# Weights split into high and low part: GpSimd's subtraction in pieces of 256 columns in place of one of 1024

## The chip, the cores and the metric

One core of a Trainium2 chip. The metric is the device time of one execution in microseconds. Five engines take part: TensorE (PE in the profile) with its own loader of weights (PEld), VectorE (DVE), ScalarE (ACT), GpSimd (POOL) and SyncE (SP, here only a queue of transfers).

## The reference, cut to what matters

The model is a chain of two blocks on 512 tokens of width 1024: two layers that mix a short convolution with a retention of four heads and have a wide MLP, and after them one layer of neighbourhood attention with a gated convolutional MLP. Nearly all of the work is in dense products in float32:

```python
proj = h @ w_in
...
return (b * z) @ w_out              # convolution mixer
...
return (jax.nn.silu(g) * o) @ w_out # retention mixer
...
x = x + merged @ w_o
h2 = rmsnorm(x, norm_mlp)
return x + jnp.square(jax.nn.relu(h2 @ w_up)) @ w_down
```

The second block adds `q`, `k`, `v`, `w_o`, `w_up` and `w_down` of the attention layer in the same manner.

## The kernel before, in words

Each float32 operand of a dense product is kept as two float32r parts, a high part (a rounded copy) and a low part (the operand minus its high part), and a product is three matmuls: high by high, high by low and low by high (`product`, line 465 on; the matmul itself is L468). Activations live in SBUF with features on the 128 partitions, in tiles of 128x512. Weights come as a stream of 404 blocks of 128x1024, each worth one job of TensorE: eight tiles of 128x128, so 24 matmuls of 512 columns into one PSUM bank.

The stream runs through a ring of four slots (`RING`), with a slot each in `w_raw`, `w_hi` and `w_lo`. For every block:

1. SyncE loads it into `w_raw` (L381) once the low part of the block four earlier is done (`w_lo_ready`).
2. ScalarE makes `w_hi` with a copy of 128x1024 (`ahead`, L864), once the block is loaded and TensorE has finished the job that used the slot (`jobs_done`).
3. GpSimd makes `w_lo` as `w_raw` minus `w_hi` (`low`, L421), once ScalarE has signalled `w_hi_ready`. This is one instruction of 128x1024 with both inputs in SBUF, and it signals `w_lo_ready`.
4. TensorE's `job` waits for `w_lo_ready` and for a free bank (`bank_free`), and runs.

So when a job ends, its slot goes through ScalarE and then GpSimd, and is wanted by TensorE three jobs later.

VectorE works on what TensorE leaves in PSUM. Between stages it splits activations: `split` casts the high part (L1117) and subtracts it (L1119), with a drain ahead of each. TensorE waits for each such tile (`tiles_ready`). Its other long stretches are: the angles of the rotary embedding at the start (L1179 to L1206), the centring and splitting of the values (L1232 to L1237), the rotary embedding of queries and keys (L1252 to L1258), the gated normalisation after retention (L1277 to L1284), the squares for the norms (L1131 to L1135), the norms (L1140 to L1148), products for the modulation of the attention layer beside the MLP (L1355, L1358), and in the last block the scaled additions of L1579 and L1615.

GpSimd has one more kind of work, in the attention layer alone: `head_biases` (L444), three subtractions of 192, 256 and 192 columns in a row with both inputs in SBUF, 16 times.

The engines' queues are written out by hand and each runs in order. There are 404 calls of `low`, most in loops over rounds of four, and 25 or so written out around the attention.

Of the kernel before, what the change touches and what calls it, by code (L numbers as in the profile page):

```python
# [22 lines left out]
F32 = mybir.dt.float32  # L23
# [3 lines left out]
ALU = mybir.AluOpType  # L27
AX_X = mybir.AxisListType.X

P = 128  # L30
# [4 lines left out]
EPS = 1e-6  # L35
RING = 4
BLK = DT * P


RH, RQK, RV = 4, 128, 256  # L40
# [137 lines left out]
def build(nc, x, ctx_in, weights, mod_weights, params, positions, decay, key_mask, rpb, block_ones, ident, out):  # L178
# [4 lines left out]
    with ctx:  # L183
# [6 lines left out]
        def at(name, offset, shape, dt=F32):  # L190
            return nc.alloc_sbuf_tensor_at(name, [P, *shape], dt, offset=base + offset)

        def pair(name, offset):

            return (at(name + "_hi", offset, [DT, S], F32R), at(name + "_lo", offset + 16 * KB, [DT, S], F32R),
                    at(name + "_hi_f", offset, [DT, S]), at(name + "_lo_f", offset + 16 * KB, [DT, S]))
# [5 lines left out]
        C_hi, C_lo, Cf, Clf = pair("C", 112 * KB)  # L202
        w_raw = at("w_raw", 144 * KB, [RING, BLK])
        w_hi = at("w_hi", 160 * KB, [RING, BLK], F32R)
        w_lo = at("w_lo", 176 * KB, [RING, BLK], F32R)
        decay_sb = at("decay_sb", 192 * KB, [RH, S])
# [13 lines left out]
        ctx_acc = at("ctx_acc", 106 * KB, [MOD_CTX, P])  # L220
        mod_w = at("mod_w", 80 * KB, [MOD_GROUP, BLK])
        ST = at("ST", 112 * KB, [3, 2, S], F32R)
# [51 lines left out]
        w_lo_ready = sem("w_lo_ready")  # L274
# [141 lines left out]
        @block.gpsimd  # L416
        def _(pool):
            def low(n, q):

                pool.wait_ge(w_hi_ready, n + 1)  # L420
                nc.gpsimd.tensor_tensor(w_lo[:, q, :], w_raw[:, q, :], w_hi[:, q, :].bitcast(F32),  # L421
                                        ALU.subtract).then_inc(w_lo_ready, 1)

            def low_rounds(first, last):
                with pool.Fori(first, last) as i:
                    for q in range(RING):
                        low(i * RING + q, q)

            low_rounds(0, ATT_ROUND)

            def head_biases(head):


                if head < 2:
                    pool.wait_ge(bias_cleared, 1)
                pool.wait_ge(toep_loaded[head % 2], (head // 2 + 1) * 16)
                if head >= BIAS_SLOTS:
                    T, a = divmod(head - BIAS_SLOTS, 2)
                    pool.wait_ge(min_ready, 2 * STEPS * T + 2 * (STEPS - 1) + a + 1)
                for kind in range(3):  # L440
                    n = REAL_KEYS[kind]
                    o = (head % BIAS_SLOTS) * BIAS_LEN + kind * KEYS + REAL[kind].start
                    t = TOEPLITZ_OFF[kind]
                    last = nc.gpsimd.tensor_tensor(  # L444
                        bias[:, o:o + n], mask_sb[:, MASK_OFF[kind]:MASK_OFF[kind] + n],
                        toeplitz[:, head % 2, t:t + n], ALU.subtract)
                last.then_inc(bias_ready, 1)

            for n in range(ATT_JOB, ATT_JOB + 3):
                low(n, n % RING)  # L450
            pool.wait_ge(late_loaded, 16 * LATE)
            for T in range(TILES):
                n = ATT_JOB + 3 * T + 3
                low(n, n % RING)
                head_biases(2 * T)
                low(n + 1, (n + 1) % RING)
                head_biases(2 * T + 1)
                low(n + 2, (n + 2) % RING)
            low(WO_JOB + 3, 3)
            low_rounds(WO_ROUND + 1, ROUNDS)  # L460
# [1291 lines left out]
```

## Time and profile before

| what | value |
|---|---|
| median of three runs | 2637.7 us (2637.61, 2637.70, 2646.06) |
| the profiled execution, its own time | 2645.72 us |
| its span (first to last instruction) | 2643.9 us |
| granted TensorE clock, mean of the span | 0.974 |
| busy share of the span: PE, DVE, ACT, POOL | 94%, 61%, 31%, 39% |
| chain that ended last, by engine | PE 78%, DVE 15%, DVEq (drains) 3%, ACT 2%, issue 2% |
| HBM traffic over the span | 93 GB/s |

The profiled execution is one run, and 8.0 us above the median. Times below are from its trace, in microseconds from the start of the span. A row of a timeline has the start, the duration, the engine, the line, the operation and its operands, and in brackets how long the engine had been idle and what ended that. A duration of VectorE or GpSimd runs from the instruction's start to its end, and holds whatever it waited for once it had started.

### The profile page before, as it was taken

How to read it: one execution, taken by the hardware profiler on the slowest of the kernel's cores; microseconds unless marked ns; L12 is line 12 of the kernel's file. 1: busy time of each engine (PE TensorE's matmuls, PEld its weight loads, DVE VectorE, ACT ScalarE, POOL GpSimd, SP SyncE). 2: the span in 40 equal slices, each digit the busy share in tenths (PEclk: the TensorE clock that was granted, in tenths of full speed). 3: DMA queues.
4: the chain of work that ended last, by engine and by line, in shares of the span. 5: the costliest groups of instructions: out<-in, count | busy, mean ns of one | idle time of the engine just before them, and what ended most of it. 6: DMA issues, size and time to landing. Idle time of an engine off the chain costs nothing.

```text
span 2643.9 us, 32621 instructions
## 1 busy us (share of the span) xinstructions
PE 2488.3 (94%) x11368; PEld 2014.9 (76%) x11368; DVE 1612.3 (61%) x1793; ACT 814.4 (31%) x1076; POOL 1040.1 (39%) x456
## 2 busy tenths in 40 slices
PE   6789999989999987999999899999599998799999
PEld 4677888868888876778888688888377776588887
DVE  7965154477666878732544776668866654763534
ACT  3132222222222221322222222222367774332222
POOL 3314444434444433244444344444123223244443
PEclk9989999999999998999999999999699999899999
DMA  4202222223433322122222323333111111132322
GB/s 158 80 31 89 95 96 97 100 95 121 143 143 117 119 76 78 43 92 96 95 97 97 123 95 143 140 138 113 35 47 56 47 39 64 64 103 89 102 93 89
DMA packets 64440, 247.24 MB, mean 94 GB/s; under 512 B 7152, under 2 KB 9584, under 8 KB 63088
## 3 DMA queue, kind: packets, MB, share of 16 engines
q1 hardware_dynamic: 62064, 218.92, 24.0%
q10 hardware_dynamic: 2304, 27.38, 2.7%
q8 instruction: 43, 0.70, 0.1%
q14 instruction: 29, 0.24, 0.0%
HBM read 244.17 MB, written 2.10 MB: 93 GB/s over the span
## 4 chain that ended last, share of the span: by engine, by line
PE 78%; DVE 15%; DVEq 3%; ACT 2%; issue 2%; DMA 0%; ACTq 0%
PE ps L468 73%; DVE E L1135 2%; PE ps L705 1%; PE ps L692 1%; DVE C_lo_f L1284 1%; DVE C_lo L1119 1%; DVE E L1131 1%; PE ps L721 1%; DVEq L1278 1%; DVE A_lo L1119 1%; DVE A_hi L1117 1%; PE ps L660 1%; DVE H_lo_f L1143 1%; DVE C_hi L1117 1%; DVEq L1256 1%
## 5 line engine op out<-in xcount | busy, mean ns | idle before, releaser
L421 POOL TENSOR_TENSOR w_lo<-w_raw,w_hi 128x1024 fp32r<-128x1024 f32 x404 | 1010.2, 2503 | 1563.5 <-ACT w_hi L864 1422.0
L468 PE MATMUL ps<-H_hi,w_hi 128*128 128x512 f32 x1952 | 781.8, 401 | 33.6 <-DVE H_lo L1442 14.6
L468 PE MATMUL ps<-H_lo,w_hi 128*128 128x512 f32 x1952 | 766.8, 393 | 0.0
L468 PE MATMUL ps<-H_hi,w_lo 128*128 128x512 f32 x1952 | 766.6, 393 | 0.0
L864 ACT ACTIVATE w_hi<-w_raw 128x1024 fp32r<-128x1024 f32 x401 | 422.6, 1057 | 842.4 <-PE ps L468 800.2
L468 PEld LDWEIGHTS ps<-H_hi,w_hi 128*128 128x128 f32 x1952 | 370.3, 190 | 133.4 <-issue 45.6
L468 PEld LDWEIGHTS ps<-H_hi,w_lo 128*128 128x128 f32 x1952 | 370.5, 190 | 79.0
L468 PEld LDWEIGHTS ps<-H_lo,w_hi 128*128 128x128 f32 x1952 | 370.9, 190 | 76.2 <-issue 3.6
L468 PE MATMUL ps<-A_hi,w_hi 128*128 128x512 f32 x560 | 220.9, 394 | 5.8 <-DVE A_lo L1119 4.2
L468 PE MATMUL ps<-A_hi,w_lo 128*128 128x512 f32 x560 | 218.7, 391 | 0.0
L468 PE MATMUL ps<-A_lo,w_hi 128*128 128x512 f32 x560 | 218.7, 391 | 0.0
L468 PE MATMUL ps<-C_hi,w_hi 128*128 128x512 f32 x384 | 150.1, 391 | 4.5 <-DVE C_lo L1119 4.5
L468 PE MATMUL ps<-C_lo,w_hi 128*128 128x512 f32 x384 | 149.4, 389 | 0.0
L468 PE MATMUL ps<-C_hi,w_lo 128*128 128x512 f32 x384 | 149.4, 389 | 0.0
L1358 DVE SCALAR_TENSOR_TENSOR mod_w<-mod_w,cond 128x768 f32<-128x768 f32 x56 | 146.9, 2624 | 0.0
L1119 DVE TENSOR_TENSOR A_lo<-A_lo_f,A_hi x78 | 141.5, 1814 | 5.8
L468 PEld LDWEIGHTS ps<-A_hi,w_hi 128*128 128x128 f32 x560 | 105.5, 188 | 32.0 <-DVE A_lo L1119 7.6
L468 PEld LDWEIGHTS ps<-A_hi,w_lo 128*128 128x128 f32 x560 | 105.5, 188 | 22.4
L468 PEld LDWEIGHTS ps<-A_lo,w_hi 128*128 128x128 f32 x560 | 105.6, 189 | 21.1
L880 ACT ACTIVATE E<-ps 128x512 f32<-128x512 f32 x64 | 38.3, 598 | 240.8 <-PE ps L468 240.8
L1117 DVE CAST A_hi<-A_lo_f x78 | 99.3, 1273 | 13.2 <-issue 9.0
L1292 DVE TENSOR_TENSOR A_lo_f<-B_hi_f,ps 128x512 f32 x16 | 11.0, 687 | 148.3 <-PE ps L468 148.3
(214 smaller groups left out, 3081.1 us busy)
## 6 DMA issues: line engine op xcount, KB each, us to landing
w_raw<-weights SPq DMA_DIRECT2D x404, 512.0 KB, 3.5
mod_w<-mod_weights ACTq DMA_DIRECT2D x8, 3072.0 KB, 10.5
X<-x SPq DMA_DIRECT2D x4, 512.0 KB, 6.8
out<-X SPq DMA_DIRECT2D x8, 256.0 KB, 2.0
toeplitz<-biases SPq DMA_DIRECT2D x14, 128.0 KB, 2.2
decay_sb<-decay ACTq DMA_DIRECT2D x1, 1024.0 KB, 7.5
ctx_sb<-context SPq DMA_DIRECT2D x1, 1024.0 KB, 5.4
mask_sb<-key_mask ACTq DMA_DIRECT2D x1, 320.0 KB, 2.7
```

The source lines that it names most:

```text
L421: nc.gpsimd.tensor_tensor(w_lo[:, q, :], w_raw[:, q, :], w_hi[:, q, :].bitcast(F32), ALU.subtract).then_inc(w_lo_ready, 1)
L468: mm = nc.tensor.matmul(dst, w[l], xs[r], start=start and a == 0, stop=stop and a == 2)
L660: nc.tensor.matmul(dst, block_sb[:, :], src[:, :], start=True, stop=True).then_inc(sum_ready[kind], 1)
L692: mm = nc.tensor.matmul(ps[:, SCORE_BANKS[head], :], (q_hi, q_lo)[l][rows, T % 2, i * P:(i + 1) * P], (k_hi, k_lo)[r][rows, first:first + ...
L705: mm = nc.tensor.transpose(ps[:, TURN_BANK, c * P:(c + 1) * P], prob[:, head, at_col:at_col + P], ident_sb[:, :])
L721: nc.tensor.matmul(ps[cols[head], OUT_BANK, o0:o0 + 2 * P], v_sb[:, T % 2, tile, cols[head]], pt[:, head, c, :, :].rearrange("p t n -> p ( ...
L864: nc.scalar.activation(w_hi[:, s, :], w_raw[:, s, :], ACT.Copy).then_inc(w_hi_ready, 1)
L880: nc.scalar.activation(dst, ps[:, q, :], func).then_inc(ev_ready, 1)
L1117: V.tensor_copy(hi, whole)
L1119: V.tensor_tensor(lo, whole, hi.bitcast(F32), ALU.subtract).then_inc(ready, 1)
L1135: return V.tensor_tensor(E[:, SUMSQ, :], E[:, SUMSQ, :], E[:, 0, :], ALU.add)
L1358: step = V.scalar_tensor_tensor(out=acc, in0=mod_w[:, 0:tiles, k * P:(k + 1) * P], scalar=cond[:, k, who:who + 1], in1=acc, op0=ALU.mult, ...
```

## The change

The loop in `low` issues four subtractions of 256 columns for each block, one after the other with nothing between them, and only the last one signals `w_lo_ready`. What is computed, the order of the blocks and every wait stay as they were.

```diff
+LOW_COLS = 2 * P
...
             def low(n, q):
 
                 pool.wait_ge(w_hi_ready, n + 1)
-                nc.gpsimd.tensor_tensor(w_lo[:, q, :], w_raw[:, q, :], w_hi[:, q, :].bitcast(F32),
-                                        ALU.subtract).then_inc(w_lo_ready, 1)
+                for c in range(0, BLK, LOW_COLS):
+                    last = nc.gpsimd.tensor_tensor(w_lo[:, q, c:c + LOW_COLS], w_raw[:, q, c:c + LOW_COLS],
+                                                   w_hi[:, q, c:c + LOW_COLS].bitcast(F32), ALU.subtract)
+                last.then_inc(w_lo_ready, 1)
```

## Rows read from the trace of the kernel before

**Rows 1.** Page, part 1: busy time, share of the span, instructions of an engine.

```profile
PE 2488.3 (94%) x11368; PEld 2014.9 (76%) x11368; DVE 1612.3 (61%) x1793; ACT 814.4 (31%) x1076; POOL 1040.1 (39%) x456
```

**Rows 2.** Groups of GpSimd's instructions by shape: busy us, mean ns, idle before.

```profile
L421 POOL TENSOR_TENSOR w_lo<-w_raw,w_hi 128x1024 fp32r<-128x1024 f32 x404 | 1010.2, 2503 | 1563.5 <-ACT w_hi L864 1422.0 <-DVE stat L1505 123.3 <-ACT w_hi L896 18.1
...
L444 POOL TENSOR_TENSOR bias<-mask_sb,toeplitz 128x256 f32<-128x256 f32 x16 | 11.9, 743 | 0.0
```

**Rows 3.** Waits of TensorE: us in total, times, longest us.

```profile
PE ps L468 <- DVE A_lo L1119: 33.3, 10, 16.0
...
PE ps L490 <- DVE E L1135: 11.5, 3, 6.5
...
PE ps L468 <- POOL w_lo L421: 1.6, 1, 1.6
```

**Rows 4.** One line's instructions: durations in ns, min/median/max.

```profile
L421 POOL TENSOR_TENSOR w_lo<-w_raw,w_hi x404: 2329/2402/2946, 12.8 to 2625.6; 128x1024 fp32r<-128x1024 f32 x135
L1119 DVE TENSOR_TENSOR A_lo<-A_lo_f,A_hi x78: 691/2722/2735, 99.3 to 2608.3; - x78
```

**Rows 5.** Timeline around 720 us, at a change of stage in an MLP.

```profile
719.79 2.66 POOL L421 TENSOR_TENSOR w_lo<-w_raw,w_hi 128x1024 fp32r<-128x1024 f32 x1 [2.78 <-ACT w_hi L864]
...
720.27 2.73 DVE L1119 TENSOR_TENSOR C_lo<-C_lo_f,C_hi  x1
...
723.05 0.50 PE L468 MATMUL ps<-C_hi,w_hi 128*128 128x512 f32 x1 [0.17 <-DVE C_lo L1119]
```

**Rows 6.** Timeline, attention layer: GpSimd's three bias subtractions beside VectorE, and each alone.

```profile
1925.35 2.26 POOL L444 TENSOR_TENSOR bias<-mask_sb,toeplitz 128x192 f32<-128x192 f32 x3
1925.76 0.53 DVE L1117 CAST k_hi<-k_lo_f 128x256 fp32r<-128x256 f32 x1
1926.36 0.80 DVE L1119 TENSOR_TENSOR k_lo<-k_lo_f,k_hi 128x256 fp32r<-128x256 f32 x1
...
1942.36 0.29 DVE L1117 CAST k_hi<-k_lo_f 128x256 fp32r<-128x256 f32 x1
1942.72 0.43 DVE L1119 TENSOR_TENSOR k_lo<-k_lo_f,k_hi 128x256 fp32r<-128x256 f32 x1
...
1964.87 1.30 POOL L444 TENSOR_TENSOR bias<-mask_sb,toeplitz 128x256 f32<-128x256 f32 x2
```

**Rows 7.** Timeline of the first layer up to the retention.

```profile
36.36 2.55 DVE L1181 TENSOR_SCALAR C_hi_f<-C_hi_f,par 128x512 f32<-128x512 f32 x1
...
74.01 2.39 POOL L421 TENSOR_TENSOR w_lo<-w_raw,w_hi 128x1024 fp32r<-128x1024 f32 x1 [2.87 <-ACT w_hi L864]
...
76.87 0.68 DVE L1232 TENSOR_REDUCE small<-ps 128x2 f32<-128x512 f32 x1
...
116.28 2.02 DVE L1117 CAST A_hi<-A_lo_f  x1 [0.52 <-issue]
...
136.67 0.79 PE L468 MATMUL ps<-A_hi 128*128 128x512 f32 x1 [15.98 <-DVE A_lo L1119]
```

**Rows 8.** Timeline of the second layer up to the retention.

```profile
1037.48 1.78 DVE L1258 TENSOR_TENSOR A_lo_f<-C_hi_f 128x512 f32 x1 [0.20 <-issue]
...
1053.72 0.80 PE L468 MATMUL ps<-A_hi 128*128 128x512 f32 x1 [13.13 <-DVE A_lo L1119]
```

**Rows 9.** Timeline of TensorE at two other changes of stage.

```profile
231.02 0.50 PE L468 MATMUL ps<-C_hi,w_hi 128*128 128x512 f32 x1 [1.93 <-DVE C_lo L1119]
...
2611.11 0.50 PE L468 MATMUL ps<-A_hi,w_hi 128*128 128x512 f32 x1 [1.69 <-DVE A_lo L1119]
```

**Rows 10.** Timeline of the attention's output projection.

```profile
2233.49 2.86 DVE L1131 TENSOR_TENSOR E<-X 128x512 f32<-128x512 f32 x1
...
2235.75 2.85 POOL L421 TENSOR_TENSOR w_lo<-w_raw,w_hi 128x1024 fp32r<-128x1024 f32 x1
...
2235.86 0.50 PE L468 MATMUL ps<-A_hi,w_hi 128*128 128x512 f32 x1 [1.62 <-POOL w_lo L421]
...
2264.43 2.07 PE L490 MATMUL ps<-E,ones 128*128 128x512 f32 x2 [6.47 <-DVE E L1135]
```

## The prediction

> **What bounds the kernel now.** I read the shares of the engines first. TensorE is busy for 2488 of 2644 us, GpSimd for 39% of them [rows 1]. So at most some 155 us can be won without touching the matmuls, and a longer GpSimd has room. Then I read who TensorE waits for. GpSimd is named in one wait of its matmuls, of 1.6 us; VectorE in nearly all, as in 33.3 us for the split L1119 and 11.5 us for the sum of squares [rows 3]. What the change makes longer is almost never waited for; what may matter is what it does to VectorE.
>
> The third view, the durations of one line, shows that link. The split's subtraction takes 691 ns at best and 2722 in the median [rows 4]. The timeline shows why: GpSimd starts a subtraction at 719.79, VectorE's starts at 720.27 and ends at 723.00, 0.55 after GpSimd's end [rows 5]. VectorE stood for 2.04 us. This holds all through the trace for VectorE's casts and for its operations with two SBUF inputs; those that read PSUM keep their time. Nothing but GpSimd's w_lo lies at such places, so GpSimd's 2.4 us instruction holds something that these operations need. The question is what four short ones do to that.
>
> **GpSimd's side.** One of 1024 columns takes 2402 ns in the median [rows 4], one of 256 of the same kind 743 [rows 2]. In a row they overlap by some 0.05: the bias pair of 256 and 192 columns takes 1.30 [rows 6]. So four take 3 x 0.69 + 0.74 = 2.81, 0.41 more. Over 404 blocks that is 166 us of GpSimd, 39% to 46% busy. A block's slot is free one job ahead of the next three, about 16.3 us at 5.44 us a job; ScalarE (1.06) and GpSimd (2.81, with VectorE's operations between perhaps 4.5) use 5.6 of them. Behind the later `w_lo_ready` stand SyncE's load, as far ahead, and in the attention layer the next biases. The added time is hidden by that lead. It shows only where the ring has run dry: at 2235.86, where TensorE waits for the first block of the output projection [rows 10], and once ahead of the last attention steps.
>
> **VectorE's side: what a wait becomes.** The nearest rows are the three bias subtractions in a row, of 192, 256 and 192 columns [rows 6]. VectorE's cast at 1925.76 takes 0.53 there and 0.29 alone, its subtraction at 1926.36 takes 0.80 and 0.43 alone. The waits are 0.24 and 0.37, both ended while GpSimd was still within its three (until 1927.61). So a waiting VectorE gets in between two queued GpSimd instructions. The same is seen with w_lo itself: VectorE's L1131, started at 2233.49, ends at 2236.35, inside the w_lo that had followed at 2235.75 without a gap, and that one took 2.85 in place of 2.40 [rows 10]. I take 0.35 for each operation that meets a piece, with up to three or four met during a block: 0.35 where one waits, 0.7 to 1.0 in a dense row, against 2.04 now. The bounds are 0.2 (the cast's) and 0.7 (a whole piece each time; four then cost 2.8, more than now).
>
> **Where this reaches TensorE.** Only delays on VectorE work that TensorE ends up waiting for count. A stop of TensorE costs its idle time and about 0.27 for the slower first starts (after 723.05 [rows 5] the next comes at 723.39, where 0.227 is the rule, and the idle column leaves out part of the gap).
>
> - First layer, to the retention. VectorE works without a break from 35.9 to 136.6, with 16 such delays from the first to the last one shown [rows 7], 29.7 us in all. But the second half of the values can't start before TensorE's eighth job ends, at 72.9 (the w_lo of 74.01 less ScalarE's 1.06), or about 71.6 with 1.3 won on the first norm; VectorE now comes to it at 76.87. From there seven delays of 11.7 us become 6.0, at 0.75 for each of the eight blocks that still come. So 5.3 + 5.7 = 11. TensorE's wait of 16 us covers it.
> - Second layer, the same place. VectorE is continuous from 997.1 only, with seven delays of 9.1 us up to the one shown [rows 8]. They become about 4: 5 us, out of a wait of 13.1.
> - Gated normalisation, twice. Delays of 12 us become about 6, but TensorE loses only 1.93 + 0.27 [rows 9]: 2.2 each, 4.4.
> - MLP, eight changes from up to down: 0.17 + 0.27 [rows 5], all won, since the last tile comes 1.7 earlier: 3.5. The two changes to `w_o` have 0.28 idle: 1.1.
> - Last MLP: three changes with 1.28, 0.35 and 1.69 idle (the last one in [rows 9]), where cast and subtraction both wait for GpSimd: 1.55 + 0.62 + 1.96 = 4.1.
> - The norms. In the last MLP group of either layer VectorE comes 0.45 late to the final addition: 0.9. The norms themselves have no w_lo beside them, the ring being full: nothing.
> - Output projection. VectorE is continuous from 2232.2 to 2264.4 with 11.6 us of delays. TensorE's first job starts later, by 0.41 and by VectorE's operations let in between, 1.2 together; its last ends near 2259, and three undisturbed operations (1.15 + 0.69 + 0.69) lead to 2262 in place of 2264.4 [rows 10]: 2.4 won.
> - Ahead of the last attention steps: 0.5 lost.
>
> The sum is 11 + 5 + 4.4 + 3.5 + 1.1 + 4.1 + 0.9 + 2.4 - 0.5 = 31.9. The profiled execution took 2645.7 and would take 2613.8. The median is 8.0 below it, and the same parts hold there: 2637.7 - 31.9 = 2605.8. What is late next is VectorE's own arithmetic in the first and second layer, and TensorE elsewhere.
>
> **Two rules of the Trainium skill.** That VectorE stands until GpSimd's instruction ends is what the page "SBUF — State Buffer", section "SBUF: two separate sides", calls an exclusive lock on a shared pair of ports, held for the whole instruction; the trace agrees (2.73 for 0.69 in [rows 5]). The page "GPSIMD Engine Reference", section "2.1 Instruction dispatch", speaks against the change: a core of GpSimd starts the next instruction as soon as its own share of the last is done, so four in a row might never let go. By it the first rival below would come true; the 0.24 and 0.37 of [rows 6] speak against it.
>
> **The rivals.**
> *No gap (slower).* GpSimd's four pieces hold VectorE out from the first to the last. Each wait is then 0.41 longer than now. On the path there are 16 + 7 in the first two layers, 6 and 6 in the normalisations (their slack is gone already), 16 in MLP changes and others, 7 at the output projection: some 50 x 0.41 = 20 less some that is hidden, 15 us: 2653. It decides wherever a waiting VectorE isn't served between pieces. For it: a w_lo is written as float32r and its pieces may follow more tightly than the biases. Against it: both cases above. 0.08.
> *Every piece costs a whole piece.* VectorE gets in but waits 0.6 to 0.7 each time. In dense rows three or four waits cost 2.0 to 2.8, as now; only single waits and changes of stage win: 0 to 3 of the 16 in the two early layers, about 2 of the normalisations, 8 at the changes, 1 at the projection, in all 12 to 18. 2622. For it: 0.69 is the distance of starts. Against it: the waits read were half of that. 0.20.
> *Something else is late instead.* VectorE's waits shrink, but TensorE's place is taken by the ring: GpSimd's block with let-in operations passes 5.44 us, or TensorE's bank comes from ScalarE. Then only the changes of stage remain, 5 to 8 us: 2631. For it: GpSimd alternates with VectorE in the densest stretches. Against it: 2.81 + 3 x 0.5 is 4.3. 0.07.
> *The forecast*, 24 to 40 us won: 0.65.
>
> **How the numbers follow.** A measurement of this kernel tells about 0.5%, 13.2 us, from no change. Faster: 0.65 and 0.12 of the second rival, which lies across that bound, 0.77. Same: the rest of it and most of the third, 0.14. Slower: the first, with what is left, 0.09. The range goes from 2596 (waits of 0.2, and the early layers winning 8 more) to 2630, which takes in the second rival.
>
> **What would show it.** L1119's median should fall from 2722 to near 1050, casts and L1135 likewise. GpSimd's 1616 pieces should come 0.69 apart where alone, its busy share near 46%. TensorE's wait before the retention should fall from 16.0 to about 5 and from 13.1 to 8; those at 231 and at the changes of the MLPs should vanish. I would be wrong if L1119 stayed at 2.7 or above, or if TensorE began to wait for w_lo in the steady stretches.

## The result, and the profile after

The changed kernel takes 2606.0 us in the median of four runs (2605.4 to 2606.8), the kernel before 2637.7 beside it: a ratio of 0.9873, with a 95% interval of 0.9853 to 0.9893. Of the 31.7 us won, 31.9 had been forecast. The sum is right; two of its terms are not, and that they cancel is luck.

The runs of the kernel before are not all alike, and what follows rests on that. They fall into two groups, of 2637 to 2641 and 2643 to 2647 us (24 and 16 of the 40 runs made beside the kernels of this study). The execution that stands ahead of the prediction belongs to the upper group. The changed kernel's eight runs lie within 2602.9 to 2606.8.

The page of the changed kernel, of its parts 1, 4 and 5 (line numbers are 3 higher than before: the subtraction of the split is L1122, the matmul L471, GpSimd's w_lo L423):

```profile
PE 2477.2 (95%) x11368; PEld 2012.5 (77%) x11368; DVE 1242.3 (48%) x1793; ACT 814.9 (31%) x1076; POOL 1373.0 (53%) x1668
...
PE 88%; DVE 7%; issue 2%; DVEq 2%; ACT 1%; POOL 0%; DMA 0%; ACTq 0%; POOLq 0%
...
L423 POOL TENSOR_TENSOR w_lo<-w_raw,w_hi 128x256 fp32r<-128x256 f32 x1616 | 1343.2, 863 | 1193.8 <-ACT w_hi L867 1057.6
```

VectorE does the same 1793 instructions in 370 us less than in [rows 1], and GpSimd needs 333 us more. The chain now runs through VectorE for 7% of the span, where it was 15%. The durations of the split's subtraction, min/median/max in ns, answer to [rows 4]:

```profile
L1122 DVE TENSOR_TENSOR A_lo<-A_lo_f,A_hi x78: 691/1070/1079, 89.4 to 2569.8; - x78
```

And TensorE's waits (us in total, times, longest us) answer to [rows 3]:

```profile
PE ps L471 <- DVE A_lo L1122: 17.5, 2, 9.0
...
PE ps L493 <- DVE E L1138: 9.1, 5, 2.7
PE ps L540 <- ACT A_lo_f L937: 4.3, 2, 2.2
...
PE ps L471 <- POOL w_lo L423: 2.7, 1, 2.7
```

The ten waits for `A_lo` have become two, the ones ahead of the two retentions. The six for `C_lo` (4.5 us in all before) and the one for `B_lo` (0.3) are gone. In the timeline these two are, with the start of the output projection's second half and the norm behind it:

```profile
123.24 0.80 PE L471 MATMUL ps<-A_hi 128*128 128x512 f32 x1 [8.95 <-DVE A_lo L1122]
...
1026.70 0.79 PE L471 MATMUL ps<-A_hi 128*128 128x512 f32 x1 [8.50 <-DVE A_lo L1122]
...
2204.53 0.50 PE L471 MATMUL ps<-A_hi,w_hi 128*128 128x512 f32 x1 [2.68 <-POOL w_lo L423]
...
2229.35 1.15 PE L493 MATMUL ps<-E,ones 128*128 128x512 f32 x2 [2.72 <-DVE E L1138]
```

The prediction calls the block waited for at this place the first of the output projection. It is the fifth of its eight: the first four are multiplied ahead, inside the attention (`WO_AHEAD`), and TensorE waits when it comes to the next round of the ring.

A change of stage in an MLP, the place of [rows 5], now looks like this:

```profile
699.30 3.90 POOL L423 TENSOR_TENSOR w_lo<-w_raw,w_hi 128x256 fp32r<-128x256 f32 x4 [1.91 <-ACT w_hi L867]
699.77 1.07 DVE L1122 TENSOR_TENSOR C_lo<-C_lo_f,C_hi  x1
```

The subtraction of 0.69 us waits 0.38 for the piece in hand, not 2.04 for the block, and TensorE no longer stops there. The four pieces take 3.90 beside VectorE.

### The profile page after: what moved, and what is told of

It is laid out like the page before. It is cut to its first block, busy times and chain, and to the rows that moved or that the text cites. A ratio compares the mean times of both kernels' runs of the same rounds, so it can differ in the third digit from the quotient of the medians.

```text
span 2603.8 us, 33833 instructions
## 1 busy us (share of the span) xinstructions
PE 2477.2 (95%) x11368; PEld 2012.5 (77%) x11368; DVE 1242.3 (48%) x1793; ACT 814.9 (31%) x1076; POOL 1373.0 (53%) x1668
## 4 chain that ended last, share of the span: by engine, by line
PE 88%; DVE 7%; issue 2%; DVEq 2%; ACT 1%; POOL 0%; DMA 0%; ACTq 0%; POOLq 0%
PE ps L471 83%; PE ps L695 1%; PE ps L708 1%; DVEq L1259 1%; PE ps L724 1%; PE ps L663 1%; DVE H_lo_f L1439 1%; DVE E L1143 1%; DVE A_lo_f L1261 0%; DVE H_lo_f L1146 0%; DVE C_hi_f L1257 0%; DVE H_lo L1151 0%; DVE H_lo L1445 0%; DVE C_hi_f L1256 0%; PE ps L728 0%
## 5 line engine op out<-in xcount | busy, mean ns | idle before, releaser
L423 POOL TENSOR_TENSOR w_lo<-w_raw,w_hi 128x256 fp32r<-128x256 f32 x1616 | 1343.2, 863 | 1193.8 <-ACT w_hi L867 1057.6
L471 PE MATMUL ps<-H_hi,w_hi 128*128 128x512 f32 x1952 | 779.4, 399 | 31.3 <-DVE H_lo L1151 14.8
L471 PE MATMUL ps<-H_lo,w_hi 128*128 128x512 f32 x1952 | 764.0, 391 | 0.0
L471 PE MATMUL ps<-H_hi,w_lo 128*128 128x512 f32 x1952 | 764.0, 391 | 0.0
L471 PEld LDWEIGHTS ps<-H_hi,w_hi 128*128 128x128 f32 x1952 | 368.5, 189 | 128.8 <-issue 39.7
L471 PEld LDWEIGHTS ps<-H_hi,w_lo 128*128 128x128 f32 x1952 | 368.9, 189 | 78.4
L471 PEld LDWEIGHTS ps<-H_lo,w_hi 128*128 128x128 f32 x1952 | 369.5, 189 | 75.8 <-issue 3.6
L471 PE MATMUL ps<-A_hi,w_hi 128*128 128x512 f32 x560 | 220.0, 393 | 2.7 <-POOL w_lo L423 2.7
L471 PE MATMUL ps<-A_hi,w_lo 128*128 128x512 f32 x560 | 218.9, 391 | 0.0
L471 PE MATMUL ps<-A_lo,w_hi 128*128 128x512 f32 x560 | 218.8, 391 | 0.0
L471 PE MATMUL ps<-C_hi,w_lo 128*128 128x512 f32 x384 | 149.4, 389 | 0.0
L471 PE MATMUL ps<-C_hi,w_hi 128*128 128x512 f32 x384 | 149.4, 389 | 0.0
L471 PE MATMUL ps<-C_lo,w_hi 128*128 128x512 f32 x384 | 149.4, 389 | 0.0
L1163 DVE TENSOR_TENSOR X<-X,ps 128x512 f32<-128x512 f32 x80 | 55.0, 688 | 171.2 <-PE ps L471 171.2
L471 PEld LDWEIGHTS ps<-A_hi,w_hi 128*128 128x128 f32 x560 | 105.6, 189 | 25.9 <-POOL w_lo L423 3.1
L471 PEld LDWEIGHTS ps<-A_hi,w_lo 128*128 128x128 f32 x560 | 105.5, 188 | 22.2
L471 PEld LDWEIGHTS ps<-A_lo,w_hi 128*128 128x128 f32 x560 | 105.6, 189 | 21.5
L1361 DVE SCALAR_TENSOR_TENSOR mod_w<-mod_w,cond 128x768 f32<-128x768 f32 x56 | 84.1, 1502 | 0.0
L471 PEld LDWEIGHTS ps<-C_hi,w_hi 128*128 128x128 f32 x384 | 72.1, 188 | 15.1
L471 PEld LDWEIGHTS ps<-C_lo,w_hi 128*128 128x128 f32 x384 | 72.1, 188 | 14.9
```

The source lines that it names most:

```text
L423: last = nc.gpsimd.tensor_tensor(w_lo[:, q, c:c + LOW_COLS], w_raw[:, q, c:c + LOW_COLS], w_hi[:, q, c:c + LOW_COLS].bitcast(F32), ALU.sub ...
L471: mm = nc.tensor.matmul(dst, w[l], xs[r], start=start and a == 0, stop=stop and a == 2)
L1163: add = V.tensor_tensor(X[:, m, :], X[:, m, :], ps[:, q, :], ALU.add)
L1361: step = V.scalar_tensor_tensor(out=acc, in0=mod_w[:, 0:tiles, k * P:(k + 1) * P], scalar=cond[:, k, who:who + 1], in1=acc, op0=ALU.mult, ...
```

## The experiments

**1. The kernel before, once more.** No edit.

> The kernel before, unchanged, looked at once more: its profiled execution was 8 us above its median, and the two profiles stand 40.1 us apart where the medians stand 31.7 apart. Theory: those 8 us are TensorE's granted clock, which in the first profile fell to 1.2 GHz again at 173, at 231 and at 1146 us while TensorE had work; a run near 2637.6 lacks at least one of these stretches, has a mean clock near 0.978 and reaches the gated stage's end (the C_lo wait, 231.0 in the first profile) at most 1 us earlier relative to the retention's start other than by clock. Rival: the 8 us lie in VectorE's waits for GpSimd, which fall differently from run to run; then the clock rows are the same and the wait before the retention (16.0 us) or the sum of L1119's durations differs by several us. If the run comes out near 2646 again, the trace should repeat the first one to within 1 us at every stage.

It took 2638.5 us, span 2636.6, of the lower group. The timeline of TensorE, and the busy time of the engines in the stretch up to the retention (us, then busy us and instructions of PE, PEld, DVE, ACT and POOL, granted clock, DMA), first of this run and then of the execution shown ahead of the prediction:

```profile
131.00 0.79 PE L468 MATMUL ps<-A_hi 128*128 128x512 f32 x1 [13.26 <-DVE A_lo L1119]
...
0.00:131.00 131.00, 92.08 (x386) 74.44 (x386) 107.89 (x138) 34.35 (x38) 47.20 (x23) 0.97 0.34 120
```

```profile
0.00:136.67 136.67, 91.78 (x387) 73.18 (x387) 114.44 (x138) 34.11 (x38) 47.35 (x23) 0.95 0.32 115
```

The same 138 instructions of VectorE hold 6.6 us more of waiting in the execution that the prediction was read from, and its retention begins 5.7 later. The two run alike up to 41 us; then GpSimd's next block starts at 41.43 in the one and at 42.82 in the other, and from there VectorE's operations meet the blocks at other points. The two spans differ by 7.3 us, so the rest of the program makes only 1.6. The theory of the expectation, the clock, was wrong in the main, and its rival, VectorE's waits, explains most. The half clock at 173 us is indeed missing in this run, and the stretch from the retention to the next norm is 2.2 us shorter; 0.6 of that come back later.

**2. Two pieces, and eight.** `LOW_COLS` at 512 and at 128.

```diff
-LOW_COLS = 2 * P
+LOW_COLS = 4 * P
```

```diff
-LOW_COLS = 2 * P
+LOW_COLS = P
```

> Two subtractions of 512 columns for each block in place of four of 256. If VectorE gets in between two instructions of GpSimd and waits for what is left of the one that runs, a wait becomes 0.6 to 1.0 us (L1119's median 1.3 to 1.7 us against 2.7 before and about 1.06 with four), the MLPs' changes of stage win all they won, the early layers win about half: 20 to 27 us below the kernel before, 2611 to 2618. If only the presence of any gap counted and not its spacing, it would be as with four, 2606. If nothing got in between (the no-gap rival), it would be at or above 2638.

> Eight subtractions of 128 columns for each block. Each is some 0.45 us from start to start, so 3.5 us a block alone, against 2.8 with four and 2.4 with one: GpSimd near 62% busy. Theory: a single wait falls to about 0.2 us and up to six are met in a dense row, so a block costs VectorE 0.8 to 1.2 in dense stretches, no less than with four: 2604 to 2609, L1119's median below 0.95. Rival (each piece costs a whole piece whatever its size, so finer cuts keep winning): under 2600. Rival (the ring becomes the bound): TensorE waits for w_lo in the steady stretches and the time goes above 2612.

Two pieces took 2624.6 us, ratio 0.9946 (0.9929 to 0.9962): 13.7 won where 20 to 27 were expected, a miss. In its profile 4.3 of these lie between the last attention step and the last norm, where TensorE also had a better clock (1.00 in place of 0.66 for 10 us, see experiment 3). Eight took 2605.9, ratio 0.987 (0.9853 to 0.9886), as expected and no better than four. The stretch up to the retention in two pieces, in four and in eight, with the split's subtraction above it for two and for eight:

```profile
L1122 DVE TENSOR_TENSOR A_lo<-A_lo_f,A_hi x78: 691/1622/1628, 93.5 to 2588.5; - x78
...
0.00:129.21 129.21, 90.99 (x386) 73.69 (x387) 104.76 (x138) 34.23 (x38) 55.34 (x42) 0.96 0.35 122
```

```profile
0.00:123.24 123.24, 90.96 (x386) 73.65 (x387) 97.07 (x138) 34.24 (x38) 66.83 (x80) 0.98 0.36 127
```

```profile
L1122 DVE TENSOR_TENSOR A_lo<-A_lo_f,A_hi x78: 691/793/797, 87.7 to 2569.5; - x78
...
0.00:120.63 120.63, 91.56 (x386) 74.12 (x386) 88.01 (x138) 34.34 (x38) 84.08 (x156) 0.99 0.37 130
```

The wait of one subtraction is 2.03 us for blocks of 1024 columns, 0.93 for 512, 0.38 for 256 and 0.10 for 128. GpSimd's instructions take 2.40, some 1.27 (the shortest), 0.70 (the distance of starts) and 0.42 (experiment 4): each wait is one instruction less about a third of a microsecond. That is why two pieces disappoint. Where VectorE works without a break it meets every piece: 2 x 0.93 is still 1.86 of the 2.03 for each block, 4 x 0.38 is 1.5, 8 x 0.10 is 0.8. VectorE's busy time up to the retention falls accordingly, 107.9, 104.8, 97.1, 88.0. At a change of stage a single wait counts, and there two pieces are enough: the stops in the MLPs of the two layers are gone in that kernel, while those of the gated normalisation stay:

```profile
220.74 0.50 PE L471 MATMUL ps<-C_hi,w_hi 128*128 128x512 f32 x1 [1.76 <-DVE C_lo L1122]
```

Eight pieces bring the retention 2.6 us earlier than four, and by the first norm of the attention layer (the matmul that waits 15.63 for L1177) they are 4.7 ahead, 1837.78 against 1842.52. They lose it behind that, where TensorE waits for other engines (a product in the norm of the keys, and the output projection):

```profile
1870.34 2.08 PE L663 MATMUL ps<-sq_k,block_sb 128*128 128x512 f32 x2 [3.68 <-ACT sq_k L1008]
...
2203.20 0.56 PE L471 MATMUL ps<-A_hi,w_hi 128*128 128x512 f32 x1 [4.14 <-POOL w_lo L423]
```

The first of these is no price of the pieces. ScalarE has this tile ready 32.4 to 32.6 us behind the first norm in every profile, with whole blocks too; a TensorE that comes earlier waits longer (1.75 with four pieces, 1.97 in the repeated kernel before). What is lost is the clock: behind the 3.68 the next eight matmuls start 0.43 us apart in place of 0.23. The same is in the mixed kernel of experiment 5, with whole blocks in this layer and 3.67 here, and not in its sister with 2.27. From the first norm to the last attention step the two with the drop take 347.5 us, the sister 344.8 and the repeated changed kernel 345.6. The second wait is GpSimd's price: a block in eight pieces beside VectorE comes 1.5 us later than in four, at the one place where the ring has run dry. Behind it the clock is 0.69 for 5.5 us where it is 1.00 in the repeated changed kernel, and the norm behind comes 1.6 later still. These three parts, 1.9, 1.5 and 1.6, are the whole lead, and only the second is GpSimd's time.

**3. One stretch at a time.** Each kernel has whole blocks everywhere but in one stretch of the stream. `low_rounds` got the number of columns as an argument, and `low` makes a whole block where none is given:

```diff
-            low_rounds(0, ATT_ROUND)
+            low_rounds(0, JOB_G // RING + 1, LOW_COLS)
+            low_rounds(JOB_G // RING + 1, ATT_ROUND)
```

```diff
-            low_rounds(0, ATT_ROUND)
+            LR = LAYER_JOBS // RING
+            low_rounds(0, 5)
+            low_rounds(5, 9, LOW_COLS)
+            low_rounds(9, LR + 5)
+            low_rounds(LR + 5, LR + 9, LOW_COLS)
+            low_rounds(LR + 9, ATT_ROUND)
```

```diff
-            low_rounds(WO_ROUND + 1, ROUNDS)
+            low_rounds(WO_ROUND + 1, ROUNDS, LOW_COLS)
```

> Four pieces for the first 20 blocks alone (values, queries and keys of the first layer, and the first four after them), one piece for the other 384. By the two profiles the start of the first layer's retention comes 13.4 us earlier (136.67 to 123.24), of which 2.3 lie ahead of the first product; if the delays of VectorE there are the cause, all of it is had by these 20 blocks: 12.5 to 14.5 us less than before, some 2624, and after it the waits at the MLPs' changes (0.16 to 1.9 us) are all there again. If the gain came from something that the pieces do to the whole program (fewer drops of the clock, less traffic), it would be under 5 us.

> Four pieces of 256 columns for the 16 blocks around the gated normalisation of each of the two layers and nowhere else; every other block has one instruction of 1024. This prices the term of the gated normalisations by itself. Theory of the prediction (waits of TensorE alone): 1.93 + 0.27 in each layer, 4.4 us, less because the first norm and the first layer keep their delays: 2633 to 2634. Rival found in the traces (the stop also costs the clock): the 3.4 us at half clock that stand right behind the stop in the first profile, at 231 and at 1146, and in the repeated one, at 223 and 1138, go as well, 1.7 us each: 7.8 us, 2629 to 2631. If the waits in these places are only partly gone, because the blocks before keep VectorE late, less than 3 us are won and the half-clock stretches stay.

> Four pieces of 256 columns from the second round of the output projection to the end (the last MLP with its norm), one instruction of 1024 everywhere before. By the lead that the changed kernel gained between the norm before the last MLP and its end (4.06), and the net gain at the output projection (1.65, of which the later start of its first block is not in this kernel, so 2 to 3): 6 to 7 us won, 2631 to 2632.5. The prediction's own terms for this part are 4.1 and 2.4, 6.5 us. The rival: the gains at the end exist only because earlier stages shifted the phase between VectorE and GpSimd; then less than 4 us are won and stops of over 1 us stay in the last MLP.

*The first 20 blocks*: 2630.7 us, ratio 0.9967 (0.9955 to 0.998), 7.7 won where 12.5 to 14.5 were expected, a miss: the expectation counted from the execution with the late retention. The retention begins at 123.40, as in the changed kernel, 7.6 ahead of the repeated kernel before. The six runs lie within 2630.4 to 2632.1. In all seven kernels of this study with pieces in these blocks, 34 runs, those of one kernel lie within 1.3 to 5.5 us; the two below with whole blocks there scatter over 9.0 and 13.5, as the kernel before does over 9.6. So the upper group comes from these blocks.

*The gated normalisations*: 2632.3 us, ratio 0.9979 (0.9966 to 0.9993). This interval goes from 1.8 to 9 us and separates nothing, but the traces do. From the start of the retention to the norm behind it, the repeated kernel before takes 434.96 us in the first layer and 435.07 in the second; this one 431.11 and 431.42; the changed kernel 430.35 and 431.39. So 3.7 to 3.9 are won in each layer, where TensorE's stop is 1.94 + 0.27. The medians are 6.5 us apart, between the 4.4 and the 7.8 of the two expectations. The rest is TensorE's clock. In the repeated kernel before:

```profile
223.16 0.50 PE L468 MATMUL ps<-C_hi,w_hi 128*128 128x512 f32 x1 [1.94 <-DVE C_lo L1119]
...
224.19 0.39 PE L468 MATMUL ps<-H_lo,w_hi 128*128 128x512 f32 x1
...
225.10 0.63 PE L468 MATMUL ps<-H_lo,w_hi 128*128 128x512 f32 x1
...
223.10:228.60 5.50, 5.44 (x17) 4.32 (x18) 0.69 (x2) 1.06 (x1) 2.36 (x1) 0.69 0.07 28
```

Right behind the stop the matmuls run at 0.39 us, then at 0.63, and the granted clock of the 5.5 us is 0.69: 3.4 of them are at 1.2 in place of 2.4 GHz (2 x 0.31 x 5.5), which costs half of that, 1.7. 17 matmuls are done in them, where 26 fit into the same time in the kernel with pieces in these places:

```profile
217.00:222.50 5.50, 5.50 (x26) 4.56 (x25) 1.71 (x3) 1.61 (x2) 2.95 (x4) 1.00 0.34 119
```

The kernel with two pieces shows the two parts by themselves, since it has the same stop twice, of 1.76 and 1.75 us, in the first layer with the drop of the clock behind it and in the second without:

```profile
220.70:226.20 5.50, 5.46 (x17) 4.34 (x18) 0.69 (x1) 1.06 (x1) 2.51 (x2) 0.69 0.19 76
1135.10:1140.60 5.50, 5.48 (x24) 4.56 (x25) 0.69 (x1) 1.06 (x1) 2.54 (x2) 1.00 0.20 80
```

Seven matmuls of 0.23 us are the clock's part, 1.6 us. The stop of 1.9 had it in both layers of both profiles of the kernel before, and again in both layers of the other two kernels of this experiment, which keep it; that of 1.69 at the end of the last MLP had not (24 matmuls, clock 1.00). So a stop of this length can cost the clock or not, and what decides is not shown; removing it takes the risk away.

*The output projection and the last MLP*: 2634.4 us in the median, 4.4 under that of the kernel before; 7.1 by the ratio, 0.9973 (0.9959 to 0.9987), which compares the means. 6 to 7 were expected. Both kernels scatter over 9 us, so the whole times say little, and the profiled execution is one with a late retention (137.11). None of the last MLP's stops is left. But it too waits 2.68 for w_lo in the output projection, as in the changed kernel: contrary to what the expectation says, the block waited for is the first of the loop that was changed. The whole span from the last attention step (the matmul with 2.96 idle) to the end takes 423.4 to 423.5 in four profiles with whole blocks there, 414.4 in this one, 416.7 and 415.6 in two profiles of the changed kernel. From the last norm to the end the three profiles with pieces agree to 0.1 us (374.4). What differs is the clock right behind the last attention step, ahead of the first block in pieces; the repeated kernel before, then this one:

```profile
2213.22:2223.22 10.00, 9.31 (x43) 6.26 (x44) 1.38 (x2) 1.76 (x3) 0.00 (x0) 0.66 0.01 2
2218.21:2228.21 10.00, 9.31 (x55) 7.20 (x56) 2.46 (x3) 2.77 (x5) 0.00 (x0) 1.00 0.01 2
```

At 1.00 the waiting block of the output projection starts 13.6 us after that step although it waits longer for w_lo; it is 15.4 in the kernel before and 16.4 and 17.5 in the changed one (clock 0.66 and 0.54). Here the clock falls behind the wait of 2.68 instead (0.69 for 5.5 us), and the norm comes 26.4 us later in place of 24.8. Most of the gain is given back so, and 1.2 of the 9.0 us are the clock's.

**4. The wait by itself.** A small kernel: GpSimd subtracts 8 blocks of 1024 columns in one go, in instructions of 1024, 256 or 128 columns, while VectorE makes 24 operations of 128x512.

```python
for i in range(8):
    for c in range(i * 1024, (i + 1) * 1024, cols):
        f = c % 1024
        last = nc.gpsimd.tensor_tensor(low[:, c:c + cols], a[:, f:f + cols], b[:, f:f + cols], ALU.subtract)
```

> It computes nothing of the reference: thirteen short phases in which GpSimd subtracts 8 blocks of 1024 columns in a row, in instructions of 1024, 256 or 128 columns, while VectorE makes 24 operations of 128x512, each drained or back to back, with both inputs in SBUF, with one in PSUM, or as a cast. Theory (a waiting VectorE gets in at the end of the GpSimd instruction in hand): beside instructions of 1024 VectorE's subtraction takes up to 2.4 + 0.69, about 2.8 to 3.1 in the mean; beside 256 columns 1.0 to 1.4; beside 128 columns 0.8 to 1.1; one with an input in PSUM keeps 0.69 and lets GpSimd keep its 0.74. Back to back operations of VectorE give the same, since GpSimd gets in between them too. Rival 1 (no gap): the first subtraction of VectorE beside 256 columns lasts until all 32 pieces are done, over 15 us. Rival 2 (a whole piece each time): 0.69 + 0.69, 1.38 in each. GpSimd's own price, without VectorE: 2.4 for 1024, 0.74 for 256 with starts 0.69 apart, and by the line through these two some 0.46 for 128, starts 0.4 apart.

GpSimd alone, with 1024, 256 and 128 columns (busy us, mean ns; the third phase is 27.0 us for 64 instructions):

```profile
L59 POOL TENSOR_TENSOR low<-a,b 128x1024 f32<-128x1024 f32 x8 | 18.9, 2395 | 8.3 <-DVE own L69 8.3
...
L59 POOL TENSOR_TENSOR low<-a,b 128x256 f32<-128x256 f32 x32 | 22.4, 750 | 0.1
...
L59 POOL TENSOR_TENSOR low<-a,b 128x128 f32<-128x128 f32 x64 | 27.0, 510 | 0.1
```

Both at once, VectorE subtracting in SBUF with a drain behind each (us; busy us and instructions of DVE, of POOL; clock, DMA), in the same order:

```profile
77.39:111.60 34.21, 32.45 (x24) 22.07 (x8) 1.00 0.00 0
111.62:144.30 32.68, 24.95 (x24) 32.63 (x32) 1.00 0.00 0
144.36:181.70 37.34, 18.74 (x24) 37.26 (x64) 1.00 0.00 0
```

Beside 256 columns one subtraction of VectorE takes 24.95 / 24 = 1.04, a wait of 0.35, which is the value that the prediction had taken. Beside whole blocks only eight of the 24 can meet one, at 2.68 by that estimate ((32.45 - 16 x 0.69) / 8), so the mean is 1.35 where 2.8 to 3.1 had been expected. Beside 128 columns it is 0.78. Without the drains the mean is 1.21 for 256 columns, a wait of 0.5. With an input in PSUM nothing waits on either side:

```profile
L59 POOL TENSOR_TENSOR low<-a,b 128x256 f32<-128x256 f32 x32 | 21.9, 731 | 0.1
L79 DVE TENSOR_TENSOR own<-ps,vb 128x512 f32<-128x512 f32 x24 | 16.6, 692 | 7.7 <-POOL low L59 6.0
```

The casts beside 256 columns take 0.80 in the mean and 0.43 alone, so they wait 0.37. No operation waited for a run of pieces (rival 1), and the mean waits stay below a whole piece of 0.70 (rival 2). The price is on GpSimd's side, and it is more than the three starts: beside a busy VectorE eight blocks take 22.1 us whole, 32.6 in 256 columns and 37.3 in 128. What VectorE no longer waits, GpSimd waits, a little each time.

**5. Mixed, and the first round of the output projection.** First with `low_rounds(0, ATT_ROUND, P)`, so pieces of 128 columns ahead of the attention, whole blocks in the attention layer and 256 columns behind it. Then the changed kernel again, together with two that have whole blocks for the last four blocks of the output projection as well, the round that TensorE waits for (the expectations call it the first):

```diff
-            low_rounds(WO_ROUND + 1, ROUNDS)
+            low_rounds(WO_ROUND + 1, WO_ROUND + 2)
+            low_rounds(WO_ROUND + 2, ROUNDS, LOW_COLS)
```

The first of these two is not the changed kernel with four blocks altered, as its expectation says: its 28 blocks made inside the attention layer are whole as well.

> A version meant to beat both: pieces of 128 columns up to the attention layer, one instruction of 1024 inside the attention layer and for the first blocks of the output projection, pieces of 256 columns after. By the leads read in the two changed kernels: the two retentions win 2.6 and 2.5 over pieces of 256, the start of the output projection loses nothing of the 2.1 that whole pieces lost there. If these parts add, 2599 to 2602. If what is won on VectorE in the early layers is given back in clock or in ScalarE's and the ring's waits, as with 128 everywhere, 2604 to 2607.

> The changed kernel itself once more, beside the two versions of this set. If its gain belongs to the change and not to one lucky profile: 2604 to 2608, and the retention of the first layer again begins at about 123.2. The profile of the changed kernel had 10 us at half clock around the start of the output projection where three others had 7, which made that start 1.0 later; if that is luck of one execution, the distance from the last attention step (the matmul with 2.96 idle) to the first matmul of the output projection is 16.4 here and not 17.5.

> The changed kernel with one instruction of 1024 columns kept for the four blocks of the first round of the output projection, where the ring has run dry and TensorE waits for the first block (2.68 us in place of 1.62). If GpSimd's added time costs there and nowhere else: that wait is 1.62 again and the matmul starts 1.06 earlier; but VectorE, which ends this stage, then waits for whole instructions again, so at most 1.1 us are won at the end and as much may be lost (in the kernel before, TensorE waited 6.5 for the norm's squares behind it, in the changed one 2.7). Time within 1.5 us of the changed kernel.

> Pieces of 128 columns up to the attention layer, whole instructions in it and for the first round of the output projection, pieces of 256 after. If the parts add, it is the gain of pieces of 128 in the two early layers (2.2 by the medians of the run with them) and up to 1.1 for the first round: 2601 to 2604. If the first round gives nothing: 2603 to 2605.

The mixed kernel took 2603.7 us (2599.8 to 2604.8), ratio 0.9857 (0.984 to 0.9875), between the sum of the parts and the other case. It too had the whole wait of 2.68 in the output projection, since the block waited for was in pieces.

The changed kernel again: 2606.2 us (2602.9 to 2606.8), its retention at 123.30. From the last attention step to the output projection it is 2204.80 - 2188.39 = 16.4, as expected, and not 17.5: the 1.1 was the clock of one execution (0.54 and 0.66 in the 10 us behind that step).

Pieces of 256 columns with whole blocks from the attention layer to the end of the output projection:

```profile
2203.57 0.50 PE L472 MATMUL ps<-A_hi,w_hi 128*128 128x512 f32 x1 [1.62 <-POOL w_lo L423]
...
2229.78 1.61 PE L494 MATMUL ps<-E,ones 128*128 128x512 f32 x2 [4.12 <-DVE E L1139]
```

The attention layer takes as long as in the repeated changed kernel (345.5 and 345.6 us from its norm to its last step), so its whole blocks changed nothing there. The matmul that waited comes 1.0 earlier after the last attention step (15.4 against 16.4), and the norm's first matmul comes 1.4 later behind it (26.2 against 24.8), since VectorE ends this stage and waits for whole blocks again. The time is 2608.3 us (2606.5 to 2609.0), 2.1 more than the changed kernel beside it where at most 1.5 either way was expected. So the later w_lo costs TensorE 1.06 there, and it is a good bargain.

The mixed kernel with this round whole took 2600.9 us (2600.2 to 2601.5), ratio 0.9842 (0.982 to 0.9863), 5.2 less than the changed kernel beside it, and no run of the one reaches the other. 2601 to 2604 had been expected if the parts add. At the first norm of the attention layer it leads by 4.45 (1838.31 against 1842.76). The whole round can't be what wins the rest, since by itself it lost a little. The profile has another source: the waiting matmul comes 13.75 us after the last attention step, and 15.39 with the same blocks in the kernel just shown, at a granted clock of 0.83 and 0.66 in the 10 us behind that step. Whether the other three runs had that clock isn't shown. Small pieces where VectorE works without a break ahead of TensorE are thus what beats four pieces everywhere; that whole blocks behind the attention help is not shown.

## Why the prediction was right, point by point

The lead of the changed kernel over the repeated kernel before, by TensorE's first matmul at each place, and what the steps of the prediction had for it:

Each row is the length in us from the place in the row above.

| stretch | before | after | won | forecast |
|---|---|---|---|---|
| start to first retention | 131.00 | 123.24 | 7.8 | 11 |
| to the norm behind it | 434.96 | 430.35 | 4.6 | 2.75 (gated 2.2, `w_o` 0.55) |
| to second retention | 480.64 | 473.11 | 7.5 | 7.2 (MLP 1.76, norm 0.45, retention 5) |
| to the norm behind it | 435.07 | 431.39 | 3.7 | 2.75 |
| to the last attention step | 731.55 | 728.97 | 2.6 | 1.7 (MLP 1.76, norm 0.45, less 0.5) |
| to the norm of the last block | 43.94 | 42.29 | 1.65 | 2.4 |
| to the end of the span | 379.44 | 374.45 | 5.0 | 4.1 |
| sum | 2636.6 | 2603.8 | 32.8 | 31.9 |

**The mechanism and its price** were right. The wait of the split's subtraction is 0.35 to 0.38 and not the 0.2 or 0.7 of the bounds; L1122's median is 1070 ns where near 1050 was forecast. The casts are where the row read was low: 0.24 for the narrow cast in [rows 6], 0.37 for one of 512 columns in experiment 4.

**First layer: the term was mis-sized against the median**, 11 where 7.8 came. The step that failed is the sentence on the 8.0 us between the profiled execution and the median, "and the same parts hold there". 5.7 of the 8.0 lay in just this part. Against the execution it was read from, 13.4 us were won. The start of the second half of the values divides what is left; it was 76.87 in [rows 7], and is, in the repeated kernel before and in the changed one:

```profile
74.26 0.69 DVE L1232 TENSOR_REDUCE small<-ps 128x2 f32<-128x512 f32 x1 [0.85 <-PE ps L468]
...
70.81 0.69 DVE L1235 TENSOR_REDUCE small<-ps 128x2 f32<-128x512 f32 x1 [4.02 <-PE ps L471]
```

That TensorE's eighth job bounds this start was right, 70.8 where about 71.6 was forecast, but the repeated kernel before reaches it 2.6 us sooner than the one that was read: 3.5 won, not 5.3. From there to the retention the delays of VectorE add up to 11.7 us in the execution read, 8.7 in the repeated one and 4.3 in the changed kernel: 4.3 won, not 5.7, although the price of 0.75 for each of eight blocks, 6.0, was too high. TensorE's wait there is 9.0 and not near 5.

**Second layer** was right as a sum with its neighbours: 8.50 idle where 8 was forecast, and 4.4 won (the lead goes from 15.5 before the second layer's first job to 19.9 at its retention), 5 forecast.

**Gated normalisations: the term was mis-sized too**, 2.2 each for 3.7 to 3.9, since it priced the stop of TensorE and not the clock behind it. Twice 1.5 to 1.7 us is most of what makes good the first layer's 3.2, which is luck. The step that failed is that the prediction counted nothing for the clock anywhere; the rows that show it (matmuls of 0.63 us a little behind the first of [rows 9]) were there to be read.

**MLPs, last MLP and norms** were right: all stops of L1119 behind up and down products are gone, and 4.06 of the last 5.0 lie between the last norm's products and the end, where 4.1 had been forecast; the other 0.9 is in the norm itself, at a better clock.

**Output projection**: its wait for w_lo 1.06 longer (1.2 forecast), 1.65 won in one profile and 2.75 in the next, on both sides of 2.4; the difference is the clock at its start (0.54 and 0.66). The kernel with pieces only there won 3.95, at 1.00. So the term is known to some 2 us only.

**GpSimd** is busy 53% and not 46%. 2.81 a block was right for a block alone; the waits that GpSimd has beside VectorE were left out of the share, although the 4.5 "with VectorE's operations between" stood in the same paragraph (3.3 in the mean, 1343 / 404). As forecast, no steady stretch waits for w_lo.

**The rivals.** That GpSimd's pieces leave no gap is refuted by experiment 4 and by L1122's 1070. The Trainium skill's page "GPSIMD Engine Reference", section "2.1 Instruction dispatch", by which a core starts its next instruction as soon as its own share of the last is done, doesn't stand against the change: whatever the cores do between instructions, VectorE gets in. Its page "SBUF — State Buffer", section "SBUF: two separate sides", with its lock for the whole instruction, agrees at every size measured: the shorter the instruction, the shorter the wait. That every piece costs a whole piece was wrong in its price, but its shape is what two pieces showed: in dense rows hardly a gain, at the changes of stage all of it. The third rival, something else late in its place, shows with eight pieces only, in GpSimd's 4.14.

What the runs leave open: when a stop of TensorE under 2 us is followed by half clock; and how much of the best version's last 0.8 is the clock at the output projection.

## What to carry to other kernels

Where VectorE's operations on SBUF are longer than they should be and GpSimd has work on SBUF beside them, look at how long one GpSimd instruction is: VectorE waits up to about that, less a third of a microsecond, once for each instruction that it meets. Where a single VectorE operation stands before a stop of TensorE, a cut in two already wins most of it; in dense stretches it gains only as the pieces get small, and GpSimd pays for it, which shows where a block is waited for. Price a stop of TensorE with the clock behind it: the 1.9 us of the gated normalisation were worth 3.7 to 3.9. And before a forecast takes the difference between a profiled execution and the median as spread evenly, look for the stretch it sits in: a second profile of the same kernel shows it.

## What the runs showed of the hardware that was not expected

- The wait of the split's subtraction, which starts within 0.1 us of the end of its cast, is nearly constant for a size (1070 ns median, 1079 the most, of 78): 2.03, 0.93, 0.38 and 0.10 us beside instructions of 1024, 512, 256 and 128 columns. Other operations wait for what is left of the instruction in hand, as the cast of 2.02 in [rows 7], 1.59 us.
- Beside a VectorE that makes one subtraction after another, with a drain behind each, GpSimd takes 4.1 us for a block of 1024 in four pieces (32.6 / 8) and 2.8 alone, but 2.8 and 2.4 for whole ones. Cutting an instruction gives the other engine more turns.
- A stop of TensorE of 1.93 us in the midst of steady work was followed by 3.4 us at half clock in both layers of four profiles with that stop, which costs 1.6 to 1.7 us more; one of 1.76 was and one of 1.75 was not, nor was one of 1.69.
- Two executions of a kernel with fixed queues can reach the same point 5.7 us apart, by how two engines fall against each other in the first 130 us. With shorter instructions there, all 34 runs lie within 1.3 to 5.5 us of the others of their kernel, where three kernels with whole blocks there scatter over 9.0 to 13.5 us.
